# Keys transposed in place in a gather ring of seven places instead of four, attention outputs stored sequence by sequence

## What is computed

```python
k_past = cache_k[page_table, :, l].reshape(DB, past, DIFF_HEADS, 2 * DIFF_DQK)
v_past = cache_v[page_table, :, l].reshape(DB, past, DIFF_HEADS, DIFF_DV)
o_diff_s = diff_attn_sample(dq, dk, dv, k_past, v_past, lam)

def diff_attn_sample(q, k_new, v_new, k_past, v_past, lam):
    s = jnp.concatenate([diff_scores(q, k_past), diff_scores(q, k_new)], axis=-1)
    w = diff_probs(s, mask, lam)      # softmax of two halves, p0 - lam * p1
    return (jnp.einsum('bhqk,bkhv->bqhv', w[..., :p], v_past)
            + jnp.einsum('bhqk,bkhv->bqhv', w[..., p:], v_new))
```

## Time and profile before

| | us |
|---|---|
| median of 3 runs (2085.1 to 2095.08) | 2092.42 |
| the profiled execution | 2101.65 |
| its span, first to last instruction | 2099.8 |
| busy in the span: TensorE, weight loads, VectorE | 1720.6, 1304.4, 1270.9 |
| busy in the span: ScalarE, GpSimd | 830.9, 412.4 |
| VectorE's 128 transposes of keys (L1326), mean of one | 294.5, 2.31 |
| GpSimd's 256 gathers (L784), mean of one | 243.9, 0.95 |

### The profile page before, as it was taken

How to read it: one execution, slowest core, us unless ns; L and a number is a source line. 1 busy time by engine, 2 the same in 40 slices (tenths; PEclk the granted TensorE clock), 3 DMA queues, 4 the chain that set the end, 5 groups by cost and what they waited for, 6 DMA issues and landing times. The chain is left out here.

```text
span 2099.8 us, 37164 instructions
## 1 busy us (share of the span) xinstructions
PE 1720.6 (82%) x14983; PEld 1304.4 (62%) x14983; DVE 1270.9 (61%) x1685; ACT 830.9 (40%) x1415; POOL 412.4 (20%) x362
## 2 busy tenths in 40 slices
PE   6999997667877877767777769952999999999990
PEld 5677776456666755555555425532788888888870
DVE  4321441777575467576766123344888898888874
ACT  4412221022212132323232132212777788778760
POOL 0000000213222233333323200004122222222203
PEclk9999999579998778888788879965999999999995
DMA  5162112859888689999998844102999999999966
GB/s 201 36 246 81 42 42 75 337 201 349 320 322 338 252 346 359 348 343 353 336 355 331 349 165 180 61 21 101 347 408 403 404 404 406 405 405 401 404 260 258
DMA packets 104800, 577.13 MB, mean 275 GB/s; under 512 B 14672, under 2 KB 20048, under 8 KB 51680
## 3 DMA queue, kind: packets, MB, share of 16 engines
q0 software_dynamic: 46512, 302.28, 38.1%
q1 hardware_dynamic: 58160, 272.98, 33.4%
HBM read 531.41 MB, written 43.81 MB: 274 GB/s over the span
## 5 line engine op out<-in xcount | busy, mean ns | idle before, releaser
L1326 DVE STREAM_TRANSPOSE d_kt<-d_ring 128x2048 f32<-128x2048 f32 x128 | 294.5, 2306 | 114.3 <-DMA d_ring<-in_cache_k,d_rows 101.7
L804 PE MATMUL ps<-d_kt,d_qb 128*32 128x128 f32 x4096 | 173.0, 322 | 162.1 <-DVE d_kt L1326 162.0
L2014 DVE TENSOR_TENSOR e_l<-first_w,e_h 128x1024 fp32r<-128x1024 f32 x256 | 294.3, 1221 | 9.9 <-ACT e_h L2011 9.8
L2011 ACT CAST e_h<-first_w 128x1024 fp32r<-128x1024 f32 x256 | 250.3, 1050 | 82.2 <-POOLq L2083 42.8
L804 PEld LDWEIGHTS ps<-d_kt,d_qb 128*32 128x32 f32 x4096 | 128.4, 128 | 200.7 <-DVE d_kt L1326 177.7
L784 POOL DMA_INDIRECT d_ring<-in_cache_k,d_rows x128 | 122.0, 953 | 582.2 <-DVE d_rows L1277 264.9
L1973 PE MATMUL ps<-e_h,e_xh 128*128 128x512 f32 x512 | 207.2, 405 | 3.5 <-DVE e_xl L2023 3.5
L1974 PE MATMUL ps<-e_l,e_xh 128*128 128x512 f32 x512 | 204.3, 399 | 0.0
L1975 PE MATMUL ps<-e_h,e_xl 128*128 128x512 f32 x512 | 204.2, 399 | 0.0
L2091 POOL COPY e_row<-order 128x1 uint32 x32 | 99.0, 3094 | 407.8 <-PE ps L1981 401.9
L784 POOL DMA_INDIRECT d_ring<-in_cache_v,d_rows x128 | 121.9, 952 | 272.0 <-PE ps L840 156.6
(11 more groups left out here) (314 smaller groups left out, 2736.2 us busy)
## 6 DMA issues: line engine op xcount, KB each, us to landing
first_w<-in_w_down SPq DMA_DIRECT2D x32, 2048.0 KB, 8.8
first_w<-in_w_up SPq DMA_DIRECT2D x62, 1024.0 KB, 7.5
first_w<-in_w_gate SPq DMA_DIRECT2D x62, 1024.0 KB, 9.8
ys_d<-e_y SPq DMA_DIRECT2D x32, 512.0 KB, 10.0
cat<-in_w_in SPq DMA_DIRECT2D x6, 2048.0 KB, 9.6
ys_d<-cat POOLq DMA_DIRECT2D x1, 8192.0 KB, 33.5
kT<-in_x_prompt SPq DMA_DIRECT2D x8, 512.0 KB, 4.4
m_wout<-in_w_out SPq DMA_DIRECT2D x2, 2048.0 KB, 10.2
```

The costliest lines, as they stand in the source:

```text
L804: mm = pe.matmul(k.ps[32 * h:32 * h + 32, SC, part], qb[:, b % 2, i, h, :], keys[:, :, h, i, :], start=i == 0, stop=i == BLOCKS - 1)
L1326: dve.transpose(kt[:, n % 2], in_ring((KEYS, b, g))).then_inc(s_kt, 1)
L2011: return act.copy(h13[:, :, kk, :], w13[:, :, kk, :])
L2014: return dve.tensor_tensor(l13[:, :, kk, :], w13[:, :, kk, :], h13[:, :, kk, :].bitcast(F32), ALU.subtract)
```

## The change

`ring` gets seven places instead of four, and the two key buffers `kt` go. VectorE transposes the keys onto themselves, in their place of the ring, without a wait for earlier scores; TensorE scores them there; and GpSimd gives a place of keys free when the scores are done (`s_sc`) instead of the transpose (`s_kt`). Memory for it also comes from elsewhere: `o` has room for two sequences instead of eight, so SP stores each sequence's output as it is ready (`store_output`), and from the third on VectorE waits until the output two before has been stored; `a_turned` becomes one buffer; `spread`, the page table and the row numbers lie in `pT` before it is used; a small buffer `mtB` goes; and the constants `spread` and `alike` are loaded by two DMAs.

```diff
-    RING, GAP = 4, 6
+    RING, GAP = 7, 6
...
-        kt = sb("d_kt", [P, 2, GROUP * W])
...
-        o = sb("d_o", [P, SAMPLES, DV])
+        o = sb("d_o", [P, 2, DV])
...
-        a_turned = sb("a_turned", [P, 2, 4, P])
+        a_turned = sb("a_turned", [P, 4, P])
...
             def _(sp):
+                def store_output(b):
+                    sp.wait_ge(s_ok, b + 1)
+                    for h in range(HEADS):
+                        for c in range(2):
+                            a = 32 * h + STEPS * c
+                            sp.dma_start(bounce[b, :, c, h, :], o[a:a + STEPS, b % 2, :]).then_inc(s_b[b % 2], 16)
...
-                sp.dma_start(spread_alike[:], io["consts"][:, KEPT:KEPT + 2 * P]).then_inc(s_con, 16)
+                sp.dma_start(spread, io["consts"][:, KEPT:KEPT + P]).then_inc(s_con, 16)
+                sp.dma_start(alike[:], io["consts"][:, KEPT + P:KEPT + 2 * P]).then_inc(s_con, 16)
...
                             sp.dma_start(new_states[e][:, b, x], h_old[DK * e:DK * e + DK, b, x]).then_inc(h_out, 16)
+                store_output(0)
                 sp.wait_ge(l_s, TILES)
...
                 sp.dma_start(dv, v_rows.rearrange("(i p) n -> p i n", p=P)).then_inc(a_dv, 16)
 
-                sp.wait_ge(s_ok, SAMPLES)
-                for h in range(HEADS):
-                    for c in range(2):
-                        a = 32 * h + STEPS * c
-                        sp.dma_start(bounce[:, :, c, h, :].rearrange("b t v -> t b v"), o[a:a + STEPS]).then_inc(s_b, 16)
-                sp.wait_ge(s_b, 16 * 2 * HEADS)
+                for b in range(1, SAMPLES):
+                    store_output(b)
+                for x in range(2):
+                    sp.wait_ge(s_b[x], 16 * HEADS * SAMPLES)
...
                     if n >= RING:
                         was, b0, x0 = loads[n - RING]
-                        pool.wait_ge(s_kt if was == KEYS else s_pv, b0 * GROUPS + x0 + 1)
+                        pool.wait_ge(s_sc if was == KEYS else s_pv, b0 * GROUPS + x0 + 1)
...
-                    keys = kt[:, n % 2].rearrange("p (r h i j) -> p r h i j", r=GROUP, h=HEADS, i=BLOCKS)
+                    keys = in_ring((KEYS, b, x)).rearrange("p (r h i j) -> p r h i j", r=GROUP, h=HEADS, i=BLOCKS)
...
-                pe.wait_ge(s_con, 16)
+                pe.wait_ge(s_con, 32)
...
-                            act.copy(a_turned[0:META, g % 2, 0, :], k.ps[0:META, ATT_T, 0:P])
+                            act.copy(a_turned[0:META, 0, :], k.ps[0:META, ATT_T, 0:P])
...
                     arrived(dve, (KEYS, b, g))
-                    if n >= 2:
-                        dve.wait_ge(s_sc, n - 1)
-                    dve.transpose(kt[:, n % 2], in_ring((KEYS, b, g))).then_inc(s_kt, 1)
+                    dve.transpose(in_ring((KEYS, b, g)), in_ring((KEYS, b, g))).then_inc(s_kt, 1)
...
-                    dve.tensor_scalar(o[:, b, :], k.ps[:, OUT, 0:DV], r2[:, 1:2], None, ALU.mult).then_inc(s_ok, 1)
+                    if b >= 2:
+                        dve.wait_ge(s_b[b % 2], 16 * 2 * HEADS * (b // 2))
+                    dve.tensor_scalar(o[:, b % 2, :], k.ps[:, OUT, 0:DV], r2[:, 1:2], None, ALU.mult).then_inc(s_ok, 1)
```

More of the change, by code:

```diff
@@ L642, in mixers @@
         ring = sb("d_ring", [P, RING, GROUP * W])
-        spread_alike = sb("d_spread_alike", [P, 2 * P])
-        spread, alike = spread_alike[:, 0:P], spread_alike[:, P:2 * P]
+        alike = sb("d_alike", [P, P])
         rows = sb("d_rows", [P, 2, SAMPLES, GROUPS], I32)
@@ L651, in mixers @@
         new_top, top = sb("d_new_top", [P, SAMPLES]), sb("d_top", [P, PIECES])
-        mt, mtT, mm8, mtB = sb("d_mt", [P, 32]), sb("d_mtT", [P, 32]), sb("d_mm8", [P, 8]), sb("d_mtB", [P, 32])
+        mt, mtT, mm8 = sb("d_mt", [P, 32]), sb("d_mtT", [P, 32]), sb("d_mm8", [P, 8])
         nm = sb("d_nm", [P, 2])
@@ L657, in mixers @@
         pTn = sb("d_pTn", [NS, P])
-        o = sb("d_o", [P, SAMPLES, DV])
+        o = sb("d_o", [P, 2, DV])
         q_pad = s[:, 0:SAMPLES * HEADS * 32].rearrange("p (b h x) -> p b h x", b=SAMPLES, h=HEADS)
         o2 = s[0:NS, 0:2 * W].rearrange("p (c n) -> p c n", c=2)
-        o_flat = o[:].rearrange("p b n -> p (b n)")
-        table = o_flat[:, 0:SAMPLES * PAGES].bitcast(I32).rearrange("p (b n) -> p b n", b=SAMPLES)
-        rows_f = o_flat[:, SAMPLES * PAGES:SAMPLES * PAGES + 2 * SAMPLES * GROUPS].rearrange("p (x b g) -> p x b g", x=2, b=SAMPLES)
+        early = pT[:].rearrange("p a r n -> p (a r n)")
+        table = early[:, 0:SAMPLES * PAGES].bitcast(I32).rearrange("p (b n) -> p b n", b=SAMPLES)
+        rows_f = early[:, 512:512 + 2 * SAMPLES * GROUPS].rearrange("p (x b g) -> p x b g", x=2, b=SAMPLES)
+        spread = early[:, 768:768 + P]
         bounce = nc.dram_tensor("d_bounce", (SAMPLES, STEPS, 2, HEADS, DV), F32, kind="Internal").ap()
@@ L687, in mixers @@
         p0 = z_flat[:, 0:2 * (META + SEQ)].rearrange("p (a n) -> p a n", a=2)
-        a_turned = sb("a_turned", [P, 2, 4, P])
-        a_flat = a_turned[:].rearrange("p a x t -> p (a x t)")
+        a_turned = sb("a_turned", [P, 4, P])
+        a_flat = a_turned[:].rearrange("p x t -> p (x t)")
         lam4 = a_flat[:, 0:4 * DK].rearrange("p (a d) -> p a d", a=4)
@@ L700, in mixers @@
                                                           sem("d_t_"), sem("d_tk"), sem("d_pv"))
-        s_ok, s_ch, s_b, s_back, s_z = sem("d_ok"), sem("d_ch"), sem("d_b"), sem("d_back"), sem("d_z")
+        s_ok, s_ch, s_b, s_back, s_z = sem("d_ok"), sem("d_ch"), [sem("d_b0"), sem("d_b1")], sem("d_back"), sem("d_z")
         l_c, l_clip, l_end, l_lo, l_q, l_k, l_turn, l_tk = (sem("g_c"), sem("g_clip"), sem("g_end"), sem("g_lo"), sem("g_q"),
@@ L825, in open_sums @@
                         pe.wait_ge(s_ok, b)
-                    pe.matmul(k.ps[:, OUT, 0:DV + PIECES], alike, sz[:, b % 2, :], start=True, stop=False, skip_group_check=True)
+                    pe.matmul(k.ps[:, OUT, 0:DV + PIECES], alike[:], sz[:, b % 2, :], start=True, stop=False, skip_group_check=True)
                     for h in range(HEADS):
@@ L1048, in prompt_values @@
                             v = k.meta_dv[:] if blk == 0 else dv[:, blk - 1, :]
-                            mm = pe.matmul(k.ps[:, ATT_O, h * DV:(h + 1) * DV], a_turned[0:w, g % 2, x, :], v[:, h * DV:(h + 1) * DV],
+                            mm = pe.matmul(k.ps[:, ATT_O, h * DV:(h + 1) * DV], a_turned[0:w, x, :], v[:, h * DV:(h + 1) * DV],
                                            start=blk == 0, stop=blk == i)
@@ L1229, in keep_probs @@
                         if first:
-                            act.copy(a_turned[0:META, g % 2, 0, :], k.ps[0:META, ATT_T, 0:P])
+                            act.copy(a_turned[0:META, 0, :], k.ps[0:META, ATT_T, 0:P])
                         b = len(blocks)
-                        act.copy(a_turned[:, g % 2, first:b, :].rearrange("p x t -> p (x t)"), k.ps[:, ATT_T, first * P:b * P]).then_inc(a_tk, 1)
+                        act.copy(a_turned[:, first:b, :].rearrange("p x t -> p (x t)"), k.ps[:, ATT_T, first * P:b * P]).then_inc(a_tk, 1)
                 def keep_attention(n):
@@ L1337, in shared_maximum @@
                     chain.link(dve.reduce_max(mm8[:], mtT[:].rearrange("p (a x) -> p x a", a=4), axis=X))
-                    chain.link(dve.transpose(mtB[:].rearrange("p (a x) -> p a x", a=4), mm8[:].unsqueeze(1).to_broadcast([P, 4, 8])))
-                    dve.tensor_scalar(nm[:, b % 2:b % 2 + 1], mtB[:, 0:1], -scale, None, ALU.mult).then_inc(s_nm, 1)
+                    chain.link(dve.transpose(mtT[:].rearrange("p (a x) -> p a x", a=4), mm8[:].unsqueeze(1).to_broadcast([P, 4, 8])))
+                    dve.tensor_scalar(nm[:, b % 2:b % 2 + 1], mtT[:, 0:1], -scale, None, ALU.mult).then_inc(s_nm, 1)
                 def output(b):
```

## The result

| | before | changed |
|---|---|---|
| median | 2093.75 us (4 runs) | 1991.99 us (4 runs, 1986.99 to 2001.47) |
| profiled execution, its span | 2101.65, 2099.8 us | 1993.27, 1991.4 us |
| ratio, 95% interval | | 0.9524 (0.9477 to 0.9572) |

What follows compares the result with a forecast made beforehand. Linear and prompt attention were taken as bound by transfers that could run faster than the four-place ring lets them. Savings of 2 + 25 + 44 = 71 us gave 2021 us from a median of 2092.42, range 1971 to 2073.

Steps and rivals of the forecast that it cites:

- B: Linear attention in the gather stage, about 460 to 683 us; forecast 25 us saved, ends 10 and 38.
- D: Prompt attention in the gather stage, 707.2 to 1206.4 us; forecast 44 us saved, ends 9 and 76.
- late waits: Waits for gathered keys and values to land: at most 37.9 us (linear attention) and 82.3 (prompt attention) can come back.
- the price of a gather: Transfer time per gather of 1.049 MB: 2.80 us taken for the prompt attention, with 2.60 and 3.05 as ends.
- A: First sequence's keys in the gather stage, 363 to 460 us; forecast 2 us saved, ends 0 and 7.
- C: Meta scores, 128 small matmuls on TensorE between linear and prompt attention, 683 to 707.2 us; forecast no change.
- Seven never hold fewer than four and two: Ring: seven places hold at least the six groups of the old four places and two key buffers.
- Three gathers more after a stop: Ring: it fills during a stop, so three more gathers are there afterwards; 160 instead of 163 remain in prompt attention.
- First, the rate does not rise: Gather stage: scattered rows go no faster than today whatever is queued; some 22 us saved, 2070 us, chance 0.12.
- Second, the keys' hold eats the depth: Ring: keys hold places longer, so runs of keys gain one place, not three; 24 us saved, 2068 us, chance 0.14.
- Third, a longer transpose: VectorE: the transpose onto itself takes longer; at 1.5 us more, 93 us are lost, 2185 us, chance 0.05.
- Fourth, nothing deepens: Ring: gathers wait for each other elsewhere, so time stays at 2092 us, chance 0.07.

Runs made afterwards that it cites:

- four in place: The changed kernel with four ring places instead of seven, all else of the change kept: 2118.81 us, ratio 1.0132 to the kernel before.

## Why the prediction was right, and where its sizes were off

*What bounds the kernel.* Right: B and D starved for data although the DMA engines stood at 0.87 and 0.92. Of the 113.2 us that the four stretches lost, 111.3 came from these two. The late waits, named as the most that can come back, held as a bound: 37.9 us in B against 36.3 measured, 82.3 in D against 75.0. With a quarter of the bytes, single profiles, the two stretches lost 38.4 and 82.7, so here the late waits were also a nearer estimate than the sum taken from a price.

*D: forecast 44 us, with ends 9 and 76; measured 75.0.* The term that was mis-sized is the price of a gather. The forecast divided 344 GB/s by a share of 0.92 to get 374 GB/s and 2.80 us. The share does not scale like that, as the run of gathers alone shows. The transfers' own price was 2.49 us, and the expert stage's 404 GB/s, which stood in the earlier trace rows as the other end, was the nearer row. The reason given against it, scattered rows, was wrong: 8 KB rows gathered through the page table run at 422. That the same sum with 2.60 us gave 76 is partly luck: with 2.49 it gives 94, and D ended at 424.2 us, above both limits, the transfers' 405 and the compute engines' 416.5.

*B: forecast 25, with ends 10 and 38; measured 36.3.* The same price was too high, and the discount from 27 to 25 for two limits that lie close was small beside it. But with 2.49 the sum gives 67 x 2.49 + 8 = 175 us, so 48 saved; B stopped at 186.7, and at 184.6 with a quarter of the bytes, so by that single profile it is the compute engines that set the time there. TensorE needed less than its old busy time: 162.1 us for the same 3002 instructions instead of 175.6, at a granted clock of 0.97 instead of 0.91.

*A: forecast 2; measured 0.* VectorE's wait for a free key buffer is gone, but its next instruction waits for TensorE, as the text said. C: forecast 0; 1.9.

*The sum* was 71 us against 101.8 between the medians.

*Seven never hold fewer than four and two:* right, and four in place, which hold fewer, are slower than before. *Three gathers more after a stop:* about two, as an estimate. Length times GB/s gives B 70.6 gathers before and 68.4 changed, D 163.8 and 161.8; the prediction itself said one more in a run of keys and three in a run of values, and the stretches mix both. The expected sign, seven issues in a row after C, was wrong, because the ring is full by then and frees one place at a time; seven in a row came only at the start. GpSimd's two long stops:

```profile
459.44 0.94 POOL L790 DMA_INDIRECT d_ring<-in_cache_k,d_rows  x1 [16.23 <-PE ps L810]
...
670.52 0.94 POOL L790 DMA_INDIRECT d_ring<-in_cache_k,d_rows  x1 [22.11 <-PE ps L810]
```

*In place:* right, the transpose takes no longer. The group of all 128 transposes, against 2306 ns for those of D in the earlier trace rows:

```profile
L1330 DVE STREAM_TRANSPOSE d_ring<-d_ring 128x2048 f32<-128x2048 f32 x128 | 292.2, 2298 | 11.8 <-DMA d_ring<-in_cache_k,d_rows 11.1
```

*Stores per sequence at no cost:* right. SP issued 64 at a median of 0.30 us and spent its time waiting for outputs. VectorE shows no wait for a store, and TensorE waits 1.2 us for an output, as before. The stores' line, and SP's wait:

```profile
L742 SPq DMA_DIRECT2D d_bounce<-d_o x64: 239/296/1123, 547.3 to 1096.3; - x64
...
SPq L742 <- DVE d_o L1351: 547.1, 7, 118.2
```

*The rivals.* First, the rate does not rise: wrong, it rose to 400 GB/s over D, and to 422 with the gathers alone. The Trainium skill ("DMA: Bandwidth & Descriptors", Bandwidth) says that the HBM side, at about 358 GB/s, binds such transfers, and in the same section that each core gets roughly this much when both cores of the HBM domain stream. The trace disagrees with it as a ceiling for this program, which runs on one core: 400 and 422 GB/s. Second, the keys' hold eats the depth: the mechanism is there, 28 us with four places, but a sixth place in place is still worth 39 us. Third, a longer transpose: 2298 ns against 2306. Fourth, nothing deepens: GpSimd issued seven gathers in a row at the start, and the kernel is 101.8 us faster. What the last line of the forecast feared did come, TensorE and VectorE filling B and D once data is early; in D the transfers were by then almost at their own limit, too (400 of 422 GB/s).

## What to carry to other kernels

Count the places in which a transfer can land, not the buffers: here two buffers that only held copies already worked on were worth 28 us with four places and nothing that can be told with five, while two more places, made from their memory, were worth 87 (2092.68 to 2005.43). More places went on paying after the number that saturates the transfers (three on the way), and their worth falls quickly (70, 39 and some 15 us here). Take the transfers' limit from a stretch that runs at it, not from a rate divided by a busy share; and when a share reaches 0.99, shrink the bytes once before calling it the bound.

## What the runs showed of the hardware

- Gathers of 1 MiB in 128 rows of 8 KB from scattered pages: 184 GB/s with one on the way, 362 with two, 422 from three on. The DMA share with two is already 0.98; from three on it is 1.01.
- Where TensorE waited less, its granted clock, a mean over its levels of 1.2 and 2.4 GHz, was higher: 0.97 instead of 0.91 in B and 0.89 instead of 0.83 in D, and the same matmuls took less busy time (336.3 instead of 369.6 us in D). The four profiles with four to seven places have 0.82, 0.86, 0.91 and 0.89 in D, and 378.5, 353.9, 335.8 and 336.3 us. That earlier data raised the clock, and so paid twice, is the likely reading; no run changes the clock alone.
- A 32x32-block transpose of 128x2048 float32 numbers onto itself took 2298 ns, into another buffer 2306.
